# Attention in 64-query units: the second key chunk cut from 128 to 64 keys, two heads to a transpose

## The reference

```python
def block_fn(args):
    qn, kn, vn, mn = args
    s = jnp.einsum('bqhgd,bkhd->bhgqk', qn, kn).astype(jnp.float32) + pos_bias
    s = jnp.where(mn[None, None, None], s, NEG_INF)
    m = jnp.maximum(jnp.max(s, axis=-1, keepdims=True), sink)
    p = jnp.exp(s - m)
    p = p / (jnp.sum(p, axis=-1, keepdims=True) + jnp.exp(sink - m))
    return jnp.einsum('bhgqk,bkhd->bqhgd', p.astype(vn.dtype), vn)
...
return (o * jax.nn.silu(z)) @ w_out
```

## Time and profile before

| | |
|---|---|
| median of 3 runs | 1972.21 us (1972.15 to 1974.3) |
| profiled execution, its own time | 1973.21 us |
| span of the profiled execution, first to last instruction | 1971.5 us |
| mean granted TensorE clock | 0.998 of 2.4 GHz |
| PE busy | 1949.2 us (99%) |
| DVE busy | 1408.7 us (71%) |
| ACT busy | 759.6 us (39%) |
| POOL busy | 891.2 us (45%) |

### The profile page before, as it was taken

How to read it: one execution, slowest core, us unless ns; L and a number is a source line. 1 busy time by engine, 2 the same in 40 slices (tenths; PEclk the granted TensorE clock), 3 DMA queues, 4 the chain that set the end, 5 groups by cost and what they waited for, 6 DMA issues and landing times.

```text
span 1971.5 us, 23476 instructions
## 1 busy us (share of the span) xinstructions
PE 1949.2 (99%) x8916; PEld 1602.3 (81%) x8916; DVE 1408.7 (71%) x2029; ACT 759.6 (39%) x1211; POOL 891.2 (45%) x596
## 2 busy tenths in 40 slices
PE   9999999999999999999999999999999999999998
PEld 7888887788888888888887788878888888777887
DVE  6999677887777776766578777776565580597566
ACT  6323435533333333121165444342122271698112
POOL 4668835645445443222264454432121472454633
PEclk9999999999999999999999999999999999999999
DMA  4231113244455444432013233263332121000202
GB/s 157 83 118 33 47 61 118 91 155 160 155 184 174 150 171 171 158 142 101 28 44 107 84 109 140 76 242 142 118 107 75 43 59 43 22 23 22 75 11 86
DMA packets 63630, 201.21 MB, mean 102 GB/s; under 512 B 7568, under 2 KB 12832, under 8 KB 63520
## 3 DMA queue, kind: packets, MB, share of 16 engines
q1 hardware_dynamic: 51088, 161.50, 23.6%
q10 hardware_dynamic: 12432, 38.23, 5.7%
HBM read 165.08 MB, written 37.77 MB: 103 GB/s over the span
## 4 chain that ended last, share of the span: by engine, by line
PE 84%; DVE 6%; ACT 4%; POOL 3%; issue 2%; DMA 1%; SPq 0%; DVEq 0%; POOLq 0%; ACTq 0%
PE psum L1098 14%; PE psum L1100 14%; PE psum L1099 14%; PE psum L1275 10%; PE psum L1273 10%; PE psum L1274 10%; POOL temp L905 2%; PE psum L1387 1%; PE psum L1386 1%; PE psum L1385 1%; PE psum L1165 1%; ACT probs L2165 1%; PE psum L1167 1%; PE psum L1166 1%; PE psum L1497 1%
## 5 line engine op out<-in xcount | busy, mean ns | idle before, releaser
L870 POOL TENSOR_TENSOR w_lo<-w_raw,w_hi 128x1024 fp32r<-128x1024 f32 x103 | 253.5, 2473 | 428.0 <-ACT w_hi L1597 426.4
L1098 PE MATMUL psum<-norm_hi,w_hi 128*128 128x512 f32 (+1 forms) x752 | 290.5, 386 | 0.0
L1099 PE MATMUL psum<-norm_lo,w_hi 128*128 128x512 f32 (+1 forms) x752 | 289.2, 385 | 0.0
L1100 PE MATMUL psum<-norm_hi,w_lo 128*128 128x512 f32 (+1 forms) x752 | 289.2, 385 | 0.0
L1273 PE MATMUL psum<-norm_hi,w_hi 128*128 128x512 f32 x464 | 181.4, 391 | 0.6 <-DVE temp L2618 0.6
L1275 PE MATMUL psum<-norm_hi,w_lo 128*128 128x512 f32 x464 | 181.2, 391 | 0.0
L1274 PE MATMUL psum<-norm_lo,w_hi 128*128 128x512 f32 x464 | 181.0, 390 | 0.0
L2650 DVE TENSOR_TENSOR stream<-psum,stream 128x512 f32<-128x512 f32 x176 | 121.2, 690 | 78.7 <-PE psum L1100 78.7
L2301 DVE SCALAR_TENSOR_TENSOR stream<-psum,mods,stream 128x512 f32<-128x512 f32 x160 | 118.7, 749 | 81.3 <-PE psum L1100 81.3
L1098 PEld LDWEIGHTS psum<-norm_hi,w_hi 128*128 128x128 f32 x752 | 141.3, 188 | 28.4 <-issue 0.2
L1100 PEld LDWEIGHTS psum<-norm_hi,w_lo 128*128 128x128 f32 x752 | 141.3, 188 | 28.2
(11 more groups left out here) (343 smaller groups left out, 4536.6 us busy)
## 6 DMA issues: line engine op xcount, KB each, us to landing
w_raw<-in_slabs SPq DMA_DIRECT2D x141, 512.0 KB, 3.5
ada_raw<-in_ada ACTq DMA_DIRECT2D x27, 1024.0 KB, 5.0
spare_raw<-in_slabs SPq DMA_DIRECT2D x20, 512.0 KB, 4.4
ffn_y_scratch<-ffn_y SPq DMA_DIRECT2D x18, 512.0 KB, 5.0
late_raw<-in_slabs SPq DMA_DIRECT2D x14, 512.0 KB, 3.5
pair_b<-pooled_scratch SPq DMA_DIRECT2D x7, 1024.0 KB, 4.9
pool_gate_scratch<-pair_c SPq DMA_DIRECT2D x12, 512.0 KB, 4.7
sum_raw<-ffn_y_scratch SPq DMA_DIRECT2D x5, 1024.0 KB, 4.9
```

Source lines behind the costliest of these rows:

```text
L870: nc.gpsimd.tensor_tensor(WL[place][:, :], RAW[at % 2][:, :], WH[place][:, :].bitcast(f32), ALU.subtract).then_inc(slab_ready, 1)
L1098: nc.tensor.matmul(dst, wh, xh, start=n == 0, stop=False)
L1099: nc.tensor.matmul(dst, wh, xl, start=False, stop=False)
L1100: last = nc.tensor.matmul(dst, wl, xh, start=False, stop=n == len(terms) - 1)
```

## The change

A unit with sub 2 or more now has one "whole" chunk of 128 keys and one "half" chunk of 64 keys. Which 64 keys are the half depends on the parity of u. For `pos` 2 and 3 the keys are stored and scored in reversed order of 64-key blocks, so that in the probability buffer the halves of two head pairs lie side by side, and one 128x128 transpose turns both (two transposes for the half chunk rather than four). In the transposed half the first pair's 64 keys then lie on partitions 0 to 63 and the second's on 64 to 127, and the value matmuls for it take 64 rows. As values are needed on the other 64 partitions as well, a copy `VS` with swapped halves is stored (ACT, at u = 2, 14 and 20). The value matmuls have 256 columns, one side of the heads each: `V[group]` for side 0, `VS` for side 1. Two waits on `half_mixed` let PE wait for its own matmuls of the other row half. Units of sub 0 have one chunk of 64 keys ("own"), units of sub 1 one whole chunk.

With this go: casts and low parts of 128x256 for the half chunk; rows of 193 rather than 257 in `PB`; sinks written by two POOL instructions rather than one; no memsets of unused columns; a scratch row moved from `PB` to `PIECES`; reversed key copies; bias rows loaded by sixteen DMAs rather than four.

```diff
-                PB = [sb(s2, f"probs{n}", [P, 4, 2 * BLOCK + 1]) for n in range(4)]
+                PB = [sb(s2, f"probs{n}", [P, 4, WINDOW + 1]) for n in range(4)]
+                with ExitStack() as s3:
+                    PIECES = sb(s3, "late_pieces", [P, S])
+                VS = sb(s2, "values_swapped", [P, NB, P], f32r)
...
+        def parts_of(u):
+            return {0: ("own",), 1: ("whole",)}.get(u % 16, ("whole", "half"))
...
+        def key_block(u, kind):
+            return u % 16 // 2 - (kind == ("half" if u % 2 else "whole"))
...
+        def score_window(u, pos):
+            return slice(0, WINDOW - hidden(u)) if pos > 1 else slice(hidden(u), WINDOW)
...
-            for r in range(4):
-                nc.gpsimd.memset(PB[r][:, :, 0:HD] if r % 2 else PB[r][:, :, 1 + WINDOW:], 0.0)
...
             def turn(u):
-                pe.wait_ge(normed, u + 1)
-                at = 1 - u % 2
-                for chunk in range(first_chunk(u), 2):
+                pe.wait_ge(normed, normed_before(u + 1))
+                for part, kind in enumerate(parts_of(u)):
                     if u:
-                        pe.wait_ge(turned_split, chunks(u - 1, chunk + 1))
-                    for pos in range(4):
...
+                        pe.wait_ge(turned_split, turned_before(u - 1, part + 1))
+                    if kind == "half":
+                        for n in range(2):
+                            at = 2 * (WINDOW + 1) * n + 1 + BLOCK
+                            last = nc.tensor.transpose(bank[part][:, P * n:P * n + P], probs_flat(u)[:, at:at + 2 * HD],
+                                                       ident[:, :])
+                    for pos in range(4 if kind != "half" else 0):
...
             def mix_values(u):
...
+                def whole(low, side):
+                    values = VS if side else V[group]
+                    heads = slice(2 * P * side, 2 * P * side + 2 * P)
+                    return nc.tensor.matmul(bank[2][:, heads], values[:, key_block(u, "whole"), :], PT[low][:, 0, heads],
+                                            start=not both and (low, side) == (0, 0), stop=not both and (low, side) == (1, 1))
+
+                def half(low, side, start=False, stop=False):
+                    values = VS if side else V[group]
+                    rows = slice(0, HD) if side == u % 2 else slice(HD, P)
+                    return nc.tensor.matmul(bank[2][:, 2 * P * side:2 * P * side + 2 * P],
+                                            values[rows, key_block(u, "half"), :], PT[low][rows, 1, 0:2 * P],
+                                            start=start, stop=stop)
+
+                if both:
+                    half(0, 0, start=True).then_inc(half_mixed, 1)
+                whole(0, 0)
+                whole(0, 1)
+                if both:
+                    pe.wait_ge(half_mixed, halves_before(u) + 1)
+                    half(0, 1)
+                    pe.wait_ge(turned_split, turned_before(u, 2))
+                    half(1, 1).then_inc(half_mixed, 1)
+                pe.wait_ge(turned_split, turned_before(u, 1))
+                whole(1, 0)
+                last = whole(1, 1)
+                if both:
+                    pe.wait_ge(half_mixed, halves_before(u) + 2)
+                    last = half(1, 0, stop=True)
                 last.then_inc(mixed, 1)
...
             def load_bias(n):
                 group, b = divmod(n, 2)
-                act.dma_start(BIAS[HD * b:HD * b + HD, 4 * group:4 * group + 4, 0:WINDOW],
...
+                act.dma_start(BIAS[HD * b:HD * b + HD, 4 * group:4 * group + 2, 0:WINDOW],
+                              bass.AP(skew_scratch.tensor, at, [[RLEN - 1, HD], [2 * RLEN * P, 2], [1, WINDOW]])
+                              ).then_inc(bias_ready[n], 16)
+                for block in range(3):
+                    act.dma_start(BIAS[HD * b:HD * b + HD, 4 * group + 2:4 * group + 4, HD * (2 - block):HD * (3 - block)],
+                                  bass.AP(skew_scratch.tensor, at + 4 * RLEN * P + HD * block,
+                                          [[RLEN - 1, HD], [2 * RLEN * P, 2], [1, HD]])).then_inc(bias_ready[n], 16)
...
+            def swap_values(group, first, last):
+                for side in range(2):
+                    nc.scalar.copy(VS[HD * side:HD * side + HD, first:last, :],
+                                   V[group][HD - HD * side:P - HD * side, first:last, :].bitcast(f32)).then_inc(v_swapped, 1)
...
+                if u == 2:
+                    act.wait_ge(v_split, 4)
+                    swap_values(0, 0, NB)
+                if u in (14, 20):
+                    swap_values(1, 4 * (u == 20), 4 * (u == 20) + 4)
                 if 3 <= u < 35:
                     w = u - 3
-                    for chunk in range(first_chunk(w), 2):
-                        act.wait_ge(turned, chunks(w, chunk + 1))
-                        nc.scalar.copy(PT[0][:, chunk, :], bank[chunk]).then_inc(turned_hi, 1)
+                    for part, kind in enumerate(parts_of(w)):
+                        act.wait_ge(turned, turned_before(w, part + 1))
+                        nc.scalar.copy(turned_part(PT[0][:, part, :], kind), turned_part(bank[part], kind)).then_inc(turned_hi, 1)
```

More of the change, by code:

```diff
@@ L444, in build, with turned_before, halves_before, normed_before @@
         LN_ORDER = [(half, 2 * pair + e) for pair in range(MT // 2) for half in range(2) for e in range(2)]
[L446 to L452, removed]
+        def parts_of(u):
+            return {0: ("own",), 1: ("whole",)}.get(u % 16, ("whole", "half"))
+        def turned_before(u, part=0):
+            return sum(len(parts_of(w)) for w in range(u)) + min(part, len(parts_of(u)))
+        def halves_before(u):
+            return 2 * sum(len(parts_of(w)) == 2 for w in range(u))
+        def normed_before(u):
+            return u + sum(w % 16 == 1 for w in range(u))
+        def key_block(u, kind):
+            return u % 16 // 2 - (kind == ("half" if u % 2 else "whole"))
+        def turned_part(t, kind):
+            return t[0:HD] if kind == "own" else t[:, 0:2 * P] if kind == "half" else t
+        def swaps_before(u):
+            return 2 if u < 16 else 4 if u < 24 else 6
         def sum_place(n, half):
@@ L1484, in turn @@
                     last.then_inc(turned, 1)
             def mix_values(u):
-                group, rest = divmod(u, 16)
-                blk = rest // 2
-                pe.wait_ge(turned_hi, chunks(u + 1))
+                group, kinds = u // 16, parts_of(u)
+                pe.wait_ge(turned_hi, turned_before(u + 1))
                 if u >= 1:
                     pe.wait_ge(o_read, u)
-                for part in range(2):
-                    for chunk in range(first_chunk(u), 2):
-                        if part:
-                            pe.wait_ge(turned_split, chunks(u, chunk + 1))
-                        last = nc.tensor.matmul(bank[2], V[group][:, blk - 1 + chunk, :], PT[part][:, chunk, :],
-                                                start=(part, chunk) == (0, first_chunk(u)), stop=(part, chunk) == (1, 1))
+                    pe.wait_ge(v_swapped, swaps_before(u))
@@ new lines, in mix_values @@
+                if kinds == ("own",):
+                    nc.tensor.matmul(bank[2], V[group][0:HD, key_block(u, "own"), :], PT[0][0:HD, 0, :], start=True, stop=False)
+                    pe.wait_ge(turned_split, turned_before(u + 1))
+                    nc.tensor.matmul(bank[2], V[group][0:HD, key_block(u, "own"), :], PT[1][0:HD, 0, :], start=False, stop=True
+                                     ).then_inc(mixed, 1)
+                    return
+                both = len(kinds) == 2
+                def whole(low, side):
[3 more added lines that the diff above has]
+                                            start=not both and (low, side) == (0, 0), stop=not both and (low, side) == (1, 1))
@@ L2092, in key_copy @@
                 n, side = divmod(m, 2)
-                ins = nc.scalar.copy(KD[n][HD * side:HD * side + HD, hs(half)],
-                                     bank[(t + 2 * half) % 4][HD * n:HD * n + HD, :])
+                keys = bank[(t + 2 * half) % 4][HD * n:HD * n + HD, :]
+                if side:
+                    ins = nc.scalar.copy(KD[n][HD:P, hs(1 - half)].rearrange("p (b k) -> p b k", k=HD)[:, ::-1, :],
+                                         keys.rearrange("p (b k) -> p b k", k=HD))
+                else:
+                    ins = nc.scalar.copy(KD[n][0:HD, hs(half)], keys)
                 if m == 3:
```

102 lines of the change are left out of this document (64 added, 38 removed).

## The result

Slower, as forecast, and 2.3 us below the predicted time:

| | before | after |
|---|---|---|
| median of 4 runs | 1973.08 us | 2003.33 us (2002.13 to 2003.94) |
| ratio, 95% interval | | 1.0152 (1.0139 to 1.0164) |
| span of the profiled execution | 1971.5 us | 2002.2 us |

A forecast was written before the change was run, and what follows sets the result against it. TensorE, busy 99% of the span, was taken as the bound, with ACT pacing mid-stage by 0.1 us a unit. Terms 29.7 + 1.6 - 3.9 + 1.1 + 3.5 + 1.4 = +33.4 us on 1972.2 gave 2005.6 us, range 1989 to 2012.

The forecast's parts named there:

- values and transposes, 28 units: TensorE in the attention stage: values +1.28 us a unit, less 0.22 for two fewer transposes; +29.7 us over 28 units.
- units of sub 0: Two attention units with 64-row value matmuls and transposes into 64 partitions, each taken as one visit: +1.6 us.
- waits that go: TensorE's waiting in the attention stage, 3.9 us, all vanishes as ACT needs less time per unit than TensorE: -3.9 us.
- swaps: Swapped-value copies on ACT at u = 14 and 20, ahead of the casts; 0.6 of 1.2 us shows, twice: +1.1 us.
- stall ahead of the query product: Twelve more bias issues on ACT delay the query copy, so TensorE waits before query product 1: +3.5 us.
- clock behind it: TensorE's granted clock drops after the idle time before query product 1, losing full-speed work: +1.4 us.
- The visits: TensorE's trips from 128-row to 64-row matmuls and back among the values: three a unit, 0.41 us each.
- Bias issues: Each of sixteen bias DMA issues on the ACT queue takes 0.64 us, whatever its size; lower end 0.33.
- Half-price visits: Rival: a trip to 64 rows and back costs 0.2 us on TensorE; +15 us, 1987 us; chance 0.12.
- Hidden bias loads: Rival: bias issues below about 0.46 us cause no stall or clock loss; +28.5 us, 2001 us; chance 0.27.
- Relief of ACT: Rival: 64-row value matmuls cost only their columns, ACT was the bound; -3 to -5 us, 1968 us; chance 0.09.
- That each half runs on 128 rows: Rival: the change doesn't do what it says, half matmuls run as 128 rows; given no chance of its own.

The follow-up runs named there:

- experiment 3: Changed kernel with its sixteen bias loads issued four at a time behind the query copies of product 1: 1999.10 us, ratio 1.0129.
- experiment 4: Kernel before with each 512-column value matmul split into two of 256 columns, all on 128 rows: 1974.83 us, ratio 1.0007.
- experiment 5: Changed kernel with halves on 128 rows, no half_mixed waits, no swaps at u = 14 and 20, bias loads behind product 1's query copies: 1969.11 us, ratio 0.9976.
- experiment 6: As experiment 3, with two half matmuls ahead of the next unit's scores and two behind, then the wholes; half chunk first: 1985.62 us, ratio 1.0062.
- experiment 1: Changed kernel with its half matmuls taking all 128 rows, same order, waits and swaps: 1979.55 us, ratio 1.0031.
- experiment 2: Changed kernel with all four whole matmuls before the four halves, one visit to 64 rows per unit for three: 1992.47 us, ratio 1.0094.
- experiment 7: Kernel before with only its four bias loads split into sixteen, same bytes to the same places: 1978.40 us, ratio 1.0026.

## Why the prediction was right, point by point

| step of the sum, us | predicted | measured | read from |
|---|---|---|---|
| values and transposes, 28 units | +29.7 | +26.3 | 28 x (2.07 - 0.91 - 0.22), see below |
| units of sub 0 | +1.6 | +0.5 | iterations 4 and 20 |
| waits that go | -3.9 | -3.8 | what is left of the stage's +24.6 |
| swaps | +1.1 | +1.6 | iterations 15 and 21 |
| stall ahead of the query product | +3.5 | +3.3 | timeline at 1631.77 |
| clock behind it | +1.4 | +1.7 | window 1631.7 to 1636 |
| sum | +33.4 | +29.6 | medians: +30.2 |

The forecast of the time, 2005.6 us, came nearer (2.3 us) than that of the difference (3.2 us) because the kernel before was 0.9 us slower beside the changed one than in the three runs at hand. That part is luck.

Ahead of the stage the table has 5.0 us and the two profiles differ by 6.0. The last microsecond need be no part of the change: the first scores start between 1677.4 and 1678.9 us in the kernels without the stall (before, experiments 3 to 6) and between 1682.0 and 1684.0 in those with it (the changed kernel, experiments 1, 2 and 7), so within each group they vary by more than one. The means of the two groups lie 5.4 us apart.

*The visits.* The mechanism holds in each detail that was named: bare loads behind each change, matmuls 0.1 us longer, three visits. The size is off by a tenth. The values take 1741.11 to 1743.18, 2.07 us where 2.19 was forecast (the start is the gate step's last matmul plus 0.23; the end allows for the 0.06 by which the transposes' first load stands bare). Less 0.96 for the columns, six changes cost 1.11 us, 0.37 a visit rather than 0.41. That is the term that was mis-sized, 28 x 0.12 = 3.4 us of the 3.8 by which the two sums differ. Whether the change itself is cheaper than at the scores, or a matmul next to a change costs only its 256 columns (an estimate: 256 / 2.4 GHz = 0.107 us, as 512 columns at 1.2 GHz take the 0.43 seen behind the stall) and not the 0.12 of the stream, isn't separated by these runs; with eight times 0.107 the six changes would cost 1.22, which is 0.41 a visit, the forecast.

The Trainium skill (TensorEngine Tiling (Array Packing), "Key Properties") says that changing the tiling mode drains the engine. The trace agrees: the first half matmul starts at 1741.21, 0.10 us after its place in the stream. The page gives no price; the larger part of a visit here is the two loads that can't be made ahead.

*Units of sub 0.* The transposes into 64 partitions were taken as one visit each, the upper end. TensorE's timeline of the first such unit:

```profile
1703.41 0.63 PE L1539 MATMUL psum<-ident,probs 128*64 128x128 f32 x4
1703.96 0.93 PE L1518 MATMUL psum<-keys,q_then_o 64*128 64x192 f32 x8
```

0.55 us, and four ordinary ones between 64-row work take 0.58 (1707.07 to 1707.65). Here scores stand on both sides. In the other unit the last half matmul, of 64 rows, stands ahead of them and scores behind (1774.23 to 1775.09), and its iteration (u = 19) lasts 4.22 us, the 4.47 of a full unit less 0.22 for the two transposes that it lacks, and less 0.03. In both places 64-row work stands on either side, so the array changes anyway, and the narrower transposes add nothing: the lower end, 0, was right. What they would cost behind 128-row work no run shows.

*Swaps.* At u = 14 the swap shows as 5.01 - 4.47 = 0.54 us, as forecast (0.6). At u = 20 it shows twice. TensorE's timeline:

```profile
1779.53 0.39 PE L1503 MATMUL psum<-norm_hi,w_lo 128*128 128x512 f32 x1
1780.51 0.39 PE L1561 MATMUL psum<-w_hi,w_lo 128*128 128x256 f32 x1 [0.60 <-ACT w_hi L2266]
...
1781.24 0.39 PE L1561 MATMUL psum<-w_lo 128*128 128x256 f32 x1 [0.22 <-DVE w_lo L3065]
```

and ACT's, where the swap stands ahead of the cast:

```profile
1778.59 1.26 ACT L2242 CAST values_swapped<-w_lo 64x512 fp32r<-64x512 f32 x2
1779.88 0.58 ACT L2266 CAST w_hi<-psum 128x512 fp32r<-128x512 f32 x1
```

The cast is that of unit 17, of sub 1, which has one chunk. Four transposes stand ahead of its values where a full unit has six (0.22 us less cover), and only two high matmuls ahead of the first low one, so that the low part is late as well. Iteration 21 lasts 4.24 us, and 3.12 in experiment 5, which has no swap there: 1.1 us. The prediction priced both swaps with the cover of a full unit.

*Waits that go.* ACT has its hole of 1.07 us, and no line of the unit shows TensorE waiting. The size wasn't measured by itself: 24.6 - 26.3 - 0.5 - 1.6 leaves -3.8, so the stage's part of the sum agrees by construction.

*Bias issues.* Size doesn't set their length: 0.63 us in the median for half and for a sixth of the bytes, 0.64 for the whole. The row of the same queue and source was the one to take, and the shorter issue of SP's slab loads was not. Experiment 7 shows that the number of issues alone makes the term; experiment 3 that it is separate from the rest. The 0.46 us that the prediction gave as the issue time below which the stall goes doesn't follow from its own terms: 12 issues of 0.35 us plus their gaps fit into the 1627.51 of the earlier trace rows, and 0.46 would still leave 1.3 us. At 0.63 nothing hangs on it.

*The clock.* The prediction's 1.4 us stopped reading at 1092.00 us, where TensorE was still at 1.2 GHz. Over 1088 to 1094 us the granted clock of the kernel before averages 0.72, and (1.00 - 0.72) x 6 = 1.7 us, as much as behind the longer hole of the changed kernel. The term was right in kind and 0.3 too small from its own rows.

*The rivals.* Half-price visits are out by the row at 1742.38. Hidden bias loads are out by the hole at 1631.77. Relief of ACT exists and is worth 4.4 us, while the costs come to eight times that (30.2 + 4.4). That each half runs on 128 rows is out by its own label, 64\*128. (The terms beside the visits in the half-price sum add up to 6.3 and not 6.7; its 1987 us stands.)

**What stays open.** A kernel that keeps the shorter chunk and never leaves 128 rows would need the half's values padded with zeros for each side; it wasn't tried. Going by experiment 5 it could gain about 4.4 us. None of the versions here beats the kernel before while computing all of the reference. How a change splits into the emptying of the array (0.10 us at 1741.21) and the bare load (0.11) is read from rows; no run has one without the other.

## What to carry to other kernels

A matmul of fewer rows isn't cheaper in a stream (512 columns on 64 rows take 0.23 us, 1706.40 to 1706.74 less 0.11 for the bare load), and each change between 128 and 64 rows cost about 0.19 us here that no row of TensorE shows as idle: count changes of rows in the order of the instructions, group them, or put them beside work that uses the same rows. Before casts and copies are made shorter, work out what that can return: the waiting that the bounding engine still has (here 4 us of 1972), not the busy time saved (here 9 us on two engines). A DMA that was cut into pieces cost its issuing engine the same time for each piece (0.63 us), so look at what stands behind the issues on that queue.

## What the runs showed of the hardware that was not expected

- A wait of TensorE on its own matmul costs 0.1 us where two matmuls stand between (experiment 1), and 0.32 us where it looks back at the one directly ahead (experiment 2: 0.22 until the result is in, 0.10 for the load that stands bare). Where a change of rows follows it adds nothing to the 0.43 us of two matmuls and a change.
- Transposes into 64 of 128 partitions (128\*64) between 64-row matmuls cost no more than ordinary ones in the same place (0.55 against 0.58 us for four).
- A hole of 3.1 us in TensorE is followed by 3.4 us at 1.2 GHz, in the changed kernel and in experiment 7 alike: 1.7 us lost. The hole of 2.35 us of the earlier trace rows, with eight matmuls of one column ahead of it, cost the same 1.7: a shorter hole wasn't cheaper.
